# Rounded operand buffers moved by 32 bytes in each partition

## The reference

```python
h = rms_norm(x, norm1_g) * (1.0 + sc1) + sh1
proj = h @ w_in
merged = gates0 * y_conv + gates1 * y_hgrn + gates2 * y_sb
x = x + g1 * (merged @ w_out)
h2 = rms_norm(x, norm2_g) * (1.0 + sc2) + sh2
x = x + g2 * (square(relu(h2 @ mlp_w1)) @ mlp_w2)
```

```python
x = x + 0.5 * swiglu(rms_norm(x, ffn1_norm), ffn1_w_gate, ffn1_w_up, ffn1_w_down)
proj = rms_norm(x, mix_norm) @ w_in + b_in
merged = sigmoid(g_attn) * y_attn + sigmoid(g_rnn) * y_rnn
x = x + merged @ w_out
x = x + 0.5 * swiglu(rms_norm(x, ffn2_norm), ffn2_w_gate, ffn2_w_up, ffn2_w_down)
```

## Time and profile before

| | |
|---|---|
| median of three runs | 3328.93 us |
| profiled execution | 3327.95 us |
| its span, first to last instruction | 3326.2 us |
| granted TensorE clock, mean over the span | 0.999 of 2.4 GHz |
| PE busy | 3306.1 us, 17742 matmuls |
| PE loading weights (beside the matmuls) | 2799.9 us |
| DVE, ACT, POOL busy | 2169.9, 1466.6, 2127.7 us |
| DMA | 343.36 MB, mean 103 GB/s |

### The profile page before, as it was taken

The page is one execution under the profiler, slowest core; times in us unless marked ns, Lnnn a source line. Parts: engine busy times, 40 slices in busy tenths (PEclk is TensorE's granted clock), DMA queues, the critical chain, the costliest instruction groups (busy, mean ns, idle before and its releaser), DMA issues.

```text
span 3326.2 us, 52762 instructions
## 1 busy us (share of the span) xinstructions
PE 3306.1 (99%) x17742; PEld 2799.9 (84%) x17742; DVE 2169.9 (65%) x3377; ACT 1466.6 (44%) x2025; POOL 2127.7 (64%) x2188
## 2 busy tenths in 40 slices
PE   9999999999999999999999999999999999999999
PEld 5888777888889997788888899889987888888998
DVE  8887685544478878714435877788878334248886
ACT  4365664222243335735634333433347545533333
POOL 6444445555568886653356888698876544468886
PEclk9999999999999999999999999999999999999999
DMA  6221553322232323332223323232223222223232
GB/s 224 88 70 64 168 181 108 104 95 96 97 112 94 107 82 102 102 127 70 70 84 110 108 101 114 76 114 101 101 89 109 95 102 70 83 92 111 102 109 99
DMA packets 94485, 343.36 MB, mean 103 GB/s; under 512 B 10609, under 2 KB 11249, under 8 KB 93954
## 3 DMA queue, kind: packets, MB, share of 16 engines
q1 hardware_dynamic: 86978, 312.11, 27.4%
q10 hardware_dynamic: 7360, 29.29, 2.7%
HBM read 335.03 MB, written 2.13 MB: 101 GB/s over the span
## 4 chain that ended last, share of the span: by engine, by line
PE 52%; POOL 23%; issue 18%; DVE 2%; ACT 2%; DVEq 1%; POOLq 0%; ACTq 0%; DMA 0%
POOL w_lo L588 22%; PE ps L634 15%; PE ps L636 15%; PE ps L635 15%; POOL t_lo L588 1%; PE ps L1217 1%; PE ps L1199 1%; PE ps L801 1%; PE ps L802 1%; PE ps L803 1%; DVE arena L2771 1%; PE ps L1208 0%; DVEq L2773 0%; ACT w_hi L1305 0%; DVE arena L2172 0%
## 5 line engine op out<-in xcount | busy, mean ns | idle before, releaser
L588 POOL TENSOR_TENSOR w_lo<-raw,w_hi 128x256 fp32r<-128x256 f32 (+1 forms) x1680 | 1467.9, 904 | 1051.9 <-ACT w_hi L1305 1049.8
L634 PE MATMUL ps<-a_hi,w_lo 128*128 128x512 f32 (+1 forms) x2720 | 1019.3, 375 | 0.8 <-DVE a_lo L2118 0.3
L636 PE MATMUL ps<-a_hi,w_hi 128*128 128x512 f32 (+1 forms) x2720 | 1005.6, 370 | 0.0
L635 PE MATMUL ps<-a_lo,w_hi 128*128 128x512 f32 (+1 forms) x2720 | 1005.3, 370 | 0.0
L588 POOL TENSOR_TENSOR w_lo<-arena,w_hi 128x512 fp32r<-128x512 f32 x384 | 586.0, 1551 | 124.7 <-ACT w_hi L1785 121.3
L634 PEld LDWEIGHTS ps<-a_hi,w_lo 128*128 128x128 f32 x2720 | 512.6, 188 | 101.0 <-issue 18.3
L1305 ACT ACTIVATE w_hi<-raw 128x1024 fp32r<-128x1024 f32 x374 | 392.6, 1053 | 442.5 <-PE ps L636 424.0
L636 PEld LDWEIGHTS ps<-a_hi,w_hi 128*128 128x128 f32 x2720 | 512.6, 188 | 88.1
L635 PEld LDWEIGHTS ps<-a_lo,w_hi 128*128 128x128 f32 x2720 | 513.0, 189 | 81.2 <-issue 0.5
L634 PE MATMUL ps<-b_hi,w_lo 128*128 128x512 f32 x1088 | 425.9, 391 | 4.8 <-DVE b_lo L2190 4.0
L635 PE MATMUL ps<-b_lo,w_hi 128*128 128x512 f32 x1088 | 424.0, 390 | 0.0
(11 more groups left out here) (332 smaller groups left out, 4706.3 us busy)
## 6 DMA issues: line engine op xcount, KB each, us to landing
raw<-in_stream SPq DMA_DIRECT2D x471, 512.0 KB, 3.3
arena<-in_stream SPq DMA_DIRECT2D x96, 512.0 KB, 3.3
arena<-in_mod_w ACTq DMA_DIRECT2D x32, 512.0 KB, 4.2
arena<-in_mod_w SPq DMA_DIRECT2D x16, 512.0 KB, 11.6
arena<-arena ACTq DMA_DIRECT2D x16, 256.0 KB, 3.7
arena<-cum_rows ACTq DMA_DIRECT2D x2, 2048.0 KB, 9.2
xres<-in_x_t SPq DMA_DIRECT2D x4, 512.0 KB, 5.4
arena<-in_first SPq DMA_DIRECT2D x8, 256.0 KB, 11.8
```

What stands on the lines that cost most here:

```text
L588: last = pool.tensor_tensor(to[:, at], of[:, at], hi[:, at].bitcast(F32), ALU.subtract)
L634: pe.matmul(out, lo, x_hi, start=start, stop=False)
L635: pe.matmul(out, hi, x_lo, start=False, stop=False)
L636: return pe.matmul(out, hi, x_hi, start=False, stop=stop)
```

## The change

Two buffers of 8 floats (32 bytes) in each partition, which no instruction uses, are declared before a_hi and behind b_lo. a_hi, a_lo, b_hi and b_lo begin 32 bytes further (38048, 54432, 70816 and 87200: 32 modulo 64). xres and all behind it begin 64 bytes further, so where they were modulo 64. raw, w_hi and w_lo don't move. No instruction is added or taken away.

```diff
         w_hi = sb("w_hi", [P, RING, D], F32R)
         w_lo = sb("w_lo", [P, RING, D], F32R)
 
+        sb("shift_operands", [P, 8])
         a_hi, a_lo = sb("a_hi", [P, KT, S], F32R), sb("a_lo", [P, KT, S], F32R)
         b_hi, b_lo = sb("b_hi", [P, KT, S], F32R), sb("b_lo", [P, KT, S], F32R)
+        sb("shift_back", [P, 8])
         xres = sb("xres", [P, KT, S])
```

## The result

The changed kernel takes 3380.4 us (median of 4 runs, 3379.95 to 3382.37) beside 3328.62 us before (median of 4): a ratio of 1.0157, 95% interval 1.0144 to 1.0170, +51.8 us. The forecast was 3377. The profiled execution took 3382.37 us, its span is 3380.7 us, 54.5 us over the one of before.

What follows compares the result with a forecast made beforehand. PE was taken to bound the kernel: +52.4 us on 512-wide matmuls and -4.1 us on 256-wide ones gave +48.3 us, 3376.3 from the profiled execution, 3377.2 from the median, stated as 3377; 8 in 10 range 3297 to 3396.

Steps and rivals of the forecast that it cites:

- PE bounds, a nanosecond per matmul reaches the end: TensorE, whole kernel: PE waits for nobody, so one nanosecond on the start distance moves the end by the number of matmuls.
- The 512-wide matmuls on a and b decide: 9888 matmuls of 512 columns on a and b: each loses 5.3 ns, at 232, for +52.4 us.
- two rows that contradict each other: For 512-wide a and b: 256-wide rows gave a 2.7 ns gain (-26.7 us), the sq_split pair an 8.3 ns loss (+82 us).
- rival A: All 11424 products: place of the start gives 2.7 ns at any width, -30.8 us, 3298; sq_split slow through its weights; chance 0.23.
- The 256-wide products on a gain 2.7 ns: 1536 products of 256 columns on a get the distance of t and q: -4.1 us.
- I put nothing for them: Buffers behind b, t and q among them: moved 64 bytes, same place modulo 64, so 0 us.
- w over a: Products with w moving and a as weights: taken as 0, bounds -2.6 to +2.9 us on the 960 of 256 columns.
- The sorting by place modulo 64: Matmuls sorted by moving operand's start, 0 or 32 modulo 64; a changed distance on t or q would refute it.
- An operand at 32 modulo 64 doesn't lock in that way.: Moving operands: unlocked starts gain at 256 columns and lose at 512, where 232 ns was taken between 230 and 235.
- B: 512-wide a and b: long stretches settle at 226.7 ns again; 3325, or 3329 with no effect at all, chance 0.13.
- C: 512-wide a and b: settled at the sq_split pair's 235 ns, 8.3 ns more each, +78 us, 3407; chance 0.14.
- D: Allocator: rounds each buffer up to 64 bytes, so nothing moves modulo 64; 3329, given no chance of its own.

Runs made afterwards that it cites:

- the run that keeps them near: Against the kernel before: a and b 32 bytes further as in the change, but the second unused buffer 96 bytes, so all behind b moves by 128; 3373.9 us.
- the run with 64 bytes: Against the kernel before: a_hi, a_lo, b_hi, b_lo and all behind them begin 64 bytes further; 3347.4 us, ratio 1.0055.
- uneven run with 16 bytes: Against the kernel before: a_hi, a_lo, b_hi, b_lo each grown by 128 bytes and used from 16 bytes in, all behind moved by 512; 3352.3 us.

## Why the prediction was right, and where it was not

**PE bounds, a nanosecond per matmul reaches the end.** Right. The waits stayed, 53.1 of 54.5 us are in the groups.

**The 512-wide matmuls on a and b decide, and between two rows that contradict each other the 512-wide one is to be believed.** They did decide, and the sum is close: over all 9888 the groups gained 51.8 us, 5.2 ns each, where I had 52.4 us. In a settled stretch 226.7 went to 233.3 ns, which is 6.6 where I took 5.3. The mean is lower because the beginnings of stretches, dear before, lose less: over both traces the first five matmuls of a stretch start 231.0 ns apart before and 233.0 after, from the eighteenth on 226.7 and 233.3. So a stretch takes some eighteen matmuls to settle, not the six that I read in the earlier trace rows. But the 512-wide row was no evidence. The pair on sq_split costs the same at distance 0 from everything (402 and 394 ns), so standing at 32 modulo 64 was not what made it slow; on that point rival A, which needed a pair that is slow for another reason, had the better reading. As far as the sign of the largest term rested on the pair, it was right by luck. It keeps one sound reason: that a's state in the kernel before is the cheap one at 512 columns and the dear one at 256, read from the earlier trace rows, which the run with t and q at distance 0 bears out (283 ns).

**The 256-wide products on a gain 2.7 ns.** Right: 283 went to 279 or 280, and the term of -4.1 us measured -5.2.

**"The buffers behind b move by 64 bytes and keep their place modulo 64: I put nothing for them."** This step failed. t and q lost 7.4 us in the groups and 6.5 by the run that keeps them near. Against it stood 1.1 us more gain on a at 256 columns, 0.9 by w over a (-1.7 and +0.8, for which I had 0 with bounds) and 0.6 less loss on the 9888. What is left, 4.8 us, is what the groups gained (53.1) beyond the forecast's 48.3.

**The sorting by place modulo 64.** Failed, as the prediction itself said it would be if t or q changed. It is the distance between the two operands, modulo 256: moved together, nothing (1.0004); with a and b left in place and only w moved, a went from 392 to 395 ns. In the kernel before, the rows on a, b, t and q could not tell the two sortings apart, since w lies at 0 modulo 64. The pair on sq_split could have: it lies at the same place modulo 256 as its weights and was dear all the same.

**"An operand at 32 modulo 64 doesn't lock in that way."** Failed in the half that I used for the size. The stretch at 233.3 is as regular as the one at 226.7: 20.0 ns on top of the columns instead of 13.3. It is another settled state and not the lack of one. That leaves the value between 230 and 235 that I took without its reason: 230 is a stretch on its way to settling, 235 a pair whose price has another cause, and neither shows the settled price at the new distance. That 232 came within 1.3 ns of it is luck too. (By the prediction's own terms 230 to 234 ns give 3357 to 3397 us and not 3355 to 3396; nothing hangs on it.)

**The rivals.** A (faster, 2.7 ns at every width) is refuted by 395 on the 512-wide groups. B said that a long stretch would settle at 226.7: it settles at 233.3. C, the pair's 235 in full, was right that there is a dearer settled state and 27 us too dear: it asked 8.3 ns of every matmul, where a settled one lost 6.6 and the mean 5.2, and took them from the pair, which does not show that state. D did not happen.

The Trainium skill, TensorE: Matmul & The Clock Gate, Step-by-step: what each phase is for, says that TensorE reads the moving operand and the weights through two ports of their own and that loading the next weights takes nothing from the running matmul's reads. The runs differ: with the same instructions and the activations at the same addresses, 32 bytes on w_hi and w_lo alone took the matmuls on a from 392 to 395 ns (the run with 64 bytes beside that with the weights moved). If neither read touched the other, and nothing else depended on the weights' place, that could not be. ACT, POOL and DVE are ruled out above, so I take the measurement to decide against the rule; that it is these two reads that meet is inferred and not seen.

**What stays open.** Where the two reads meet, if it is they, and why the same distance is cheap at 512 columns and dear at 256 (0: 390 and 283 ns; 32: 395 and 280). t at a distance of 64, with its own and its weights' addresses equal, took 279 to 281 beside a at 0 and 278 beside a at 32; so the neighbours have a part, as in the uneven run with 16 bytes, and its rule is not known. Nor is it known why the pair on sq_split is dear. No run beat the kernel before: its a and b stand at the best distance that was tried for 512 columns, and t and q at one that no tried placement improved without costing more elsewhere.

## What to carry to other kernels

In this kernel, where matmuls in float32r run back to back with a weight load before each, the distance between the moving and the stationary buffer modulo 256 bytes was worth 3% of a 512-wide matmul (226.7 against 233.3 ns from start to start), and 0 was the best of those tried (16, 32, 64 and 128 were not). At 256 columns 0 was among the worst, by 2 to 3% (120 ns against 117). A new small buffer ahead of such operands, or one whose length is no multiple of 256 bytes, can cost as much as it did here, 1.6% of the kernel, without touching an instruction, so pad it where the wide matmuls rule. Before a price is read off a row that is unlike the matmuls it is meant for, as the two on sq_split are, ask what else is unlike in it. And compare mean durations by form and by buffer, since the totals by engine show only that PE is busy.

## What the runs showed of the hardware that was not expected

| distance of moving from stationary, bytes modulo 256 | 512 columns, mean ns | 256 columns, mean ns |
|---|---|---|
| 0 | 390 (a, b), 389 (w over a), 392 to 402 (sq_split) | 283 to 284 (a), 283 (w over a; t and q, moved there) |
| 16 | 394 | 279 (a) |
| 32 | 395 to 396 | 279 to 280 (a; 283 once), 278 to 281 (t) |
| 64 | 392 (a), 392 to 394 (b) | 279 to 280 (a), 278 to 281 (t) |
| 96 | | 280 to 284 (t, q) |
| 128 | 395 to 396 | 281 to 282 (a) |
| 160 | | 280 (t), 280 to 281 (q) |
| 192 (w over a) | 394 | 278 |
| 224 (w over a) | 395 to 396 | 281 |
| 240 (w over a) | 394 to 397 | 281 |

The table leaves out the uneven run with 16 bytes and, of a and b at 512 columns and w over a at 256, the first of the three products, which the start of a tile lengthens. The 283 at a distance of 32 is the first product on a in the run with the weights moved; the other two took 279 and 280. Subtract 163 for the distance between two starts. Sixteen bytes are already seen. Moves by 256 and 512 bytes are not seen, to 0.1%.
